# Sparse attention reordered: selection behind the index keys, a score bank per query tile, transposed weights, sums over 512 queries

## The reference

```
c_q, c_kv, k_idx, w_idx = split(h @ w_in)       # 256, 256, 64, 8 columns; c_q, c_kv, k_idx normed
q_abs, q_idx = split(c_q @ w_uq)                # 16 heads x 256 (normed), 8 index heads x 64
act   = relu(einsum("bqhd,bsd->bqhs", q_idx, k_idx) * 64 ** -0.5)
score = einsum("bqh,bqhs->bqs", w_idx, act)     # -1e30 where the key's chunk is ahead of the query's
sel   = top_k(score, 128)                       # one set of keys for all heads
logits = q_abs . c_kv[sel] * 256 ** -0.5 + bias[rel]
p      = softmax(logits)                        # masked as above
o      = (p @ c_kv[sel]) @ w_uv[head]           # 64 columns a head
h      = h + o @ w_out
```

## Time and profile before

| | us |
|---|---|
| median of three runs | 4014.04 (4010.49 to 4017.86) |
| the profiled execution | 4015.53 |
| its span on the core | 4013.8 |
| PE busy | 3690.2 (92%), 20688 records |
| PE weight loads busy | 2999.4 (75%) |
| DVE busy | 1743.2 (43%) |
| ACT busy | 1305.5 (33%) |
| POOL busy | 353.8 (9%) |
| PE's granted clock, mean of the core | 0.961 of full speed |

### The profile page before, as it was taken

The page is one execution under the profiler, slowest core; times in us unless marked ns, Lnnn a source line. Parts: engine busy times, 40 slices in busy tenths (PEclk is TensorE's granted clock), DMA queues, the critical chain, the costliest instruction groups (busy, mean ns, idle before and its releaser), DMA issues. The chain is left out here.

```text
span 4013.8 us, 51945 instructions
## 1 busy us (share of the span) xinstructions
PE 3690.2 (92%) x20688; PEld 2999.4 (75%) x20688; DVE 1743.2 (43%) x2625; ACT 1305.5 (33%) x1827; POOL 353.8 (9%) x263
## 2 busy tenths in 40 slices
PE   8999799699999998858888999999988989799997
PEld 7999677699999998425554888888833467677886
DVE  4442366354334432254332543444248843445432
ACT  4331366243324321123332442343110044324421
POOL 0000222000000000001000000000027332230000
PEclk9999899799999999969999999999989999899999
DMA  4322311022222223000002222322222242133221
GB/s 167 125 81 84 113 48 53 14 102 94 79 99 84 94 83 113 29 12 26 1 1 74 94 95 92 106 94 88 79 69 76 69 123 64 70 109 115 94 86 70
DMA packets 115310, 318.10 MB, mean 79 GB/s; under 512 B 13335, under 2 KB 56471, under 8 KB 99060
## 3 DMA queue, kind: packets, MB, share of 16 engines
q1 hardware_dynamic: 115188, 316.48, 23.2%
HBM read 307.95 MB, written 17.01 MB: 81 GB/s over the span
## 5 line engine op out<-in xcount | busy, mean ns | idle before, releaser
L326 PE MATMUL acc<-fb_xh,fb_wh 128*128 128x264 f32 x1408 | 287.9, 286 | 11.9 <-DVE fb_wl L476 11.9
L326 PE MATMUL acc<-fb_xl,fb_wh 128*128 128x264 f32 x1408 | 288.4, 286 | 0.0
L326 PE MATMUL acc<-fb_xh,fb_wl 128*128 128x264 f32 x1408 | 287.8, 286 | 0.0
L326 PE MATMUL acc<-fd_xh,fd_wh 128*128 128x512 f32 x704 | 275.8, 392 | 10.4 <-DVE fd_wl L476 10.4
L326 PE MATMUL acc<-fd_xh,fd_wl 128*128 128x512 f32 x704 | 274.8, 390 | 0.0
L326 PE MATMUL acc<-fd_xl,fd_wh 128*128 128x512 f32 x704 | 274.8, 390 | 0.0
L326 PEld LDWEIGHTS acc<-fb_xh,fb_wh 128*128 128x128 f32 x1408 | 220.1, 189 | 12.3 <-DVE fb_wl L476 12.1
L326 PEld LDWEIGHTS acc<-fb_xl,fb_wh 128*128 128x128 f32 x1408 | 219.4, 189 | 0.0
L326 PEld LDWEIGHTS acc<-fb_xh,fb_wl 128*128 128x128 f32 x1408 | 219.1, 189 | 0.0
L397 ACT ACTIVATE fb_wh<-fb_raw 128x2048 fp32r<-128x2048 f32 (+1 forms) x74 | 124.7, 1686 | 290.0 <-PE acc L385 176.9
L471 DVE TENSOR_TENSOR fb_wl<-fb_raw,fb_wh 128x2048 fp32r<-128x2048 f32 (+1 forms) x74 | 148.3, 2004 | 141.3 <-ACT fb_wh L397 140.5
(11 more groups left out here) (537 smaller groups left out, 8716.8 us busy)
## 6 DMA issues: line engine op xcount, KB each, us to landing
fb_raw<-wi_dram SPq DMA_DIRECT2D x42, 1024.0 KB, 4.8
fd_raw<-wi_dram SPq DMA_DIRECT2D x42, 1024.0 KB, 4.8
fb_raw<-wo_dram SPq DMA_DIRECT2D x32, 704.0 KB, 4.0
fd_raw<-wo_dram SPq DMA_DIRECT2D x32, 704.0 KB, 4.0
fa_raw<-wi_dram SPq DMA_DIRECT2D x20, 1024.0 KB, 4.8
ff_raw<-wi_dram SPq DMA_DIRECT2D x20, 1024.0 KB, 4.8
a_raw<-a_qkv_dram SPq DMA_DIRECT2D x24, 512.0 KB, 4.1
s_gw<-gate_w_dram SPq DMA_DIRECT2D x24, 512.0 KB, 4.0
```

The lines of the kernel that those rows point to most:

```text
L326: last = pe.matmul(acc[:, up_base(p, b) + 2 * a + q, 0:w], x[:, k, a, :], part[:, k, t0:t0 + w], start=k == 0 and part is xh and x is wv, ...
```

## The change

In `latents` the values are no longer computed; `uv` is loaded into the not yet used `mix` buffer in the same place of SP's queue. In `latent_heads`:
- The index jobs are placed by tile (`INDEX_AT`): tile 0 ahead of head 0; six jobs of tile 1 ahead of head 2 and two ahead of head 3; tile 2 at heads 5 and 7; tile 3 at heads 10, 11 and 12. There are four relu slots, not two. The 16 rounds of a selection are written out; there is no hardware loop.
- The scores of tile t stand in bank t. The first four are issued behind the last query, and then scores(g+4) behind turn(g). The ten value jobs stand between the last sums and the first turn, on ACT behind the root of the norms, all copied by ACT.
- The exponential is written over the logits, DVE scales them in place by the reciprocal (`weigh`, now behind logit(g+1)), and `turn` is a transpose of each key tile. Key tiles are now 16 meta keys and full tiles of 128. ACT's exps run three steps ahead, behind `spread`.
- `outputs` runs once a head, over 512 queries: the meta keys, then key tile j for the queries from 128 j on. ACT stores 64 x 512 at once.

```diff
-                    pe.wait_ge(there_uv, 17)
-                    pe.wait_ge(ckv_on, 2)
-                    for n, (j, rows, half) in enumerate(blocks):
...
+            AHEAD = 6
+            INDEX_AT = {0: (0, of_tile[1]), 2: (of_tile[1], of_tile[1] + AHEAD), 3: (of_tile[1] + AHEAD, of_tile[2]),
+                        5: (of_tile[2], of_tile[2] + AHEAD), 7: (of_tile[2] + AHEAD, of_tile[3]),
+                        10: (of_tile[3], of_tile[3] + AHEAD), 11: (of_tile[3] + AHEAD, of_tile[3] + 9),
+                        12: (of_tile[3] + 9, len(jobs))}
             I_BANK = (4, 5, 6)
-            OUT_BANK = (4, 5)
-            per_head = -(-len(jobs) // 8)
+            V_BANK = (5, 6)
+            T_BANK = (5, 7)
+            O_BANK = 6
+            OUT_BANK = (0, 1)
+            v_jobs = [(j, half) for j in range(-1, QT) for half in range(2)]
...
+                    def values(n):
+                        j, half = v_jobs[n]
+                        rows, at = (META, 0) if j < 0 else (P, META + j * P)
+                        if n >= 2:
+                            pe.wait_ge(v_ev, 1 + n - 1)
...
-                                last = pe.matmul(flat[:, 2 * BANK * (g % 2) + a:2 * BANK * (g % 2) + b],
+                                last = pe.matmul(flat[:, BANK * t + a:BANK * t + b],
...
                     def turn(g):
...
-                            last = pe.matmul(to, e[:, g % 2, j * P:j * P + n], diag[:, g % 2, :], start=True, stop=True)
+                        if t == NT - 1 and hd:
+                            pe.wait_ge(mixed, 1 + hd)
+                        pd, bank = lg_of(g), T_BANK[g % 2]
+                        to = acc[0:META, bank, (t + 1) * P:(t + 2) * P] if t < NT - 1 else acc[0:META, O_BANK, 0:P]
+                        pe.transpose(to, pd[:, 0:META], ident[:, :])
+                        for j in range(t + 1):
+                            last = pe.transpose(acc[:, bank, j * P:(j + 1) * P], pd[:, META + j * P:META + (j + 1) * P],
+                                                ident[:, :])
...
+                    def outputs(hd):
...
+                        pe.wait_ge(pt_ready, 1 + NT * (hd + 1))
+                        pe.matmul(acc[0:64, O_BANK, :], valm[:, hs], ptm[0:META, u, :], start=True, stop=False)
+                        for j in range(QT):
+                            last = pe.matmul(acc[0:64, O_BANK, j * P:], vals[:, j, hs], pt[:, u, j, j * P:],
+                                             start=False, stop=j == QT - 1)
...
+                    for hd in range(B_HEADS):
+                        for n in range(*INDEX_AT.get(hd, (0, 0))):
+                            index_scores(n)
+                        query(hd)
+                        if hd:
+                            sums(hd - 1)
+                    pe.wait_ge(q_ev, 1 + B_HEADS)
+                    pe.wait_ge(relued, 1 + len(jobs))
+                    for t in range(NT):
+                        scores(t)
+                    sums(B_HEADS - 1)
+                    pe.wait_ge(uv_there, 17)
+                    for n in range(len(v_jobs)):
+                        values(n)
+                    pe.wait_ge(v_ev, 1 + len(v_jobs))
+                    for g in range(LAST):
                         hd, t = STEPS_[g]
                         turn(g)
-                        if g + 2 < LAST:
-                            scores(g + 2)
-                        if g:
-                            outputs(g - 1)
+                        if g + NT < LAST:
+                            scores(g + NT)
+                        if t == 0 and hd:
+                            outputs(hd - 1)
...
-                        if n >= 2:
-                            act.wait_ge(i_added, 1 + n - 1)
+                        if n >= 4:
+                            act.wait_ge(i_added, 1 + n - 3)
...
                     act.wait_ge(u_mean, 2)
                     act.activation(rq[:, :, :], mean_u[:, :, :], ACT.Sqrt).then_inc(u_root, 1)
+                    for n in range(len(v_jobs)):
+                        take_values(n)
+                    for g in range(3):
+                        exps(g)
+                    for g in range(LAST):
                         hd, t = STEPS_[g]
                         spread(g)
+                        if t == 1 and hd:
+                            store(hd - 1)
+                        if g + 3 < LAST:
+                            exps(g + 3)
+                    store(B_HEADS - 1)
...
-                        with dve.Fori(0, TOPK // 8):
+                        for _round in range(TOPK // 8):
...
-                        dve.tensor_scalar(diag[:, s, :], ident[:, :], rden[:, s:s + 1], None,
-                                          ALU.mult).then_inc(weights, 1)
+                        dve.tensor_scalar(lg, lg, rden[:, s:s + 1], None, ALU.mult).then_inc(weights, 1)
...
                     logit(0)
-                    logit(1)
-                    for g in range(LAST):
-                        weigh(g)
-                        if g + 2 < LAST:
-                            logit(g + 2)
+                    for g in range(1, LAST):
+                        logit(g)
+                        weigh(g - 1)
+                    weigh(LAST - 1)
```

More of the change, by code:

```diff
@@ L1382, in _, with latent_heads @@
                     last.then_inc(ckv_on, 1)
[L1383 to L1389, removed]
+        def latent_heads(st, ckv, vals, valm, g_lat, widx, eps_q, mb, mix, uv, bw, c_bw, early, uq_there, uv_there):
             q_all = sb(st, "l_q_all", [P, 2 * B_HEADS, SEQ])
-            late = sb(st, "l_late", [P, 6 * SEQ])
             top8 = sb(st, "l_top8", [P, 8])
@@ L1404, in latent_heads @@
[L1404 to L1409, removed]
+            nmx = sb(st, "l_nmx", [P, 8])
@@ L1475, in index_scores @@
                                   kidx[hs, a:b], start=True, stop=True).then_inc(i_mm, 1)
[L1477 to L1480, removed]
-                        for n in range(per_head * hd + per_head // 2, min(len(jobs), per_head * (hd + 1))):
-                            index_scores(n)
-                        if hd:
-                            sums(hd - 1)
-                    sums(B_HEADS - 1)
+                    def values(n):
[3 more added lines that the diff above has]
+                            pe.wait_ge(v_ev, 1 + n - 1)
+                        for r in range(2):
+                            last = pe.matmul(acc[0:rows, V_BANK[n % 2], :], ckv[:, r, at:at + rows],
+                                             uv[:, 8 * half:8 * half + 8, r * 64:(r + 1) * 64],
+                                             start=r == 0, stop=r == 1)
+                        last.then_inc(v_mm, 1)
                     def scores(g):
@@ L1563, in _, with take_values @@
                         last.then_inc(q_ev, 1)
-                        for n in range(per_head * hd + per_head // 2, min(len(jobs), per_head * (hd + 1))):
+                    def take_values(n):
+                        j, half = v_jobs[n]
+                        cols = slice(512 * half, 512 * half + 512)
+                        act.wait_ge(v_mm, 1 + n + 1)
+                        if j < 0:
+                            act.activation(valm[:, cols], acc[0:META, V_BANK[n % 2], :], ACT.Copy).then_inc(v_ev, 1)
+                        else:
+                            act.activation(vals[:, j, cols], acc[:, V_BANK[n % 2], :], ACT.Copy).then_inc(v_ev, 1)
```

189 lines of the change are left out of this document (91 added, 98 removed).

## The result

The changed kernel takes 3842.41 us (median of 4 runs, 3838.15 to 3844.69) where the kernel before took 4014.51 (4 runs). The ratio is 0.957, 95% interval 0.9554 to 0.9587: faster by 172 us. The forecast was 3861, so the sign, the places and most sizes were right, and 19 us more came than were promised. The profiled execution is one of 3844.69 us, span 3843.0 (before 4015.53, span 4013.8), 170.8 less.

What follows compares the result with a forecast made beforehand. PE is busy nearly everywhere, so only the front (DVE its engine) and head loop (PE waiting for DVE) could pay: 4015.5 - 50.6 (front and values) - 102 (loop) = 3862.9, less 1.5 to the median, 3861; range 3842 to 3892.

Steps and rivals of the forecast that it cites:

- the loop's sum of PE a head: Head loop: PE alone sets the pace, scores 5.6, transposes 2.34, outputs 3.2, together 11.14 us a head; loop -102.
- rival B: Front: relus ahead block ACT, query takes wait, DVE keeps 29 us more of waits; near 3890, chance 0.11.
- The lower bound of 162: Head loop: its length in us with no handoff gaps at all, against 174.4 forecast.
- Values out of the latents: Before the front: without the value product, the query stage starts 21.4 us earlier, at about 1661.4.
- DVE's chain in the front: Front: rounds, additions, clearing, thresholds and 7.5 us of waits end selection 115.6 us after the stage's start.
- PE in the front: Front: queries, index jobs, half clock and stops about 104 us, 110 with first scores and last sums; done before DVE.
- The seam: Between selection and head loop: root, value jobs and first exp put the first turn at 134.3 us, 136.3 with half clock.
- A: DVE's selection rounds: the 0.34 gap is the replace draining, so unrolling gives nothing; 3877, chance 0.12.
- C: Head loop: stays bound by the chain, PE keeps its 46.5 us of waits for DVE; 3908, chance 0.11.
- D: Head loop: transposes let the clock fall to 1.2 GHz throughout, slower than before; 4034, chance 0.03.

Runs made afterwards that it cites:

- the run with wide weights: Changed kernel with the turn as matmuls with the identity, the first of each turn taking 128 weight columns instead of 16: 3866.24 us.
- the even placement: Changed kernel with index jobs and relus placed as in the kernel before, five a head over the first eight heads: 3870.67 us.
- the shallow lead: Changed kernel with scores issued two steps ahead instead of four, and exps two ahead instead of three: 3964.04 us.

## Why the prediction was right in kind and 19 us too slow

**The step that failed is the loop's sum of PE a head, 11.14 where 9.76 was measured.** Its transposes were sized right at 0.11, but 0.2 a group was added for a handoff that isn't there: turns 1.54, not 2.34. The scores were copied start to start from the earlier trace rows, 5.6, and take 4.92 without any change to them. Outputs were 0.1 too low, 3.2 for 3.30. The first two contain the same thing. In the kernel before nearly every neighbour has weights of another shape (128*128 in scores and turn, 128*16 at a turn's end, 128*64 and 16*64 in outputs), and each such seam costs 0.10 to 0.14 us in the runs above. Its trace had the row that shows it, beside the first scores of the earlier trace rows:

```profile
1969.09 0.76 PEld L1493 LDWEIGHTS acc<-b_ckv,l_q_all 128*128 128x128 f32 x4 [0.21 <-issue]
```

Load and matmul both start at 1969.09. I had read this "issue" as a price of each group. The 0.2 for a group of transposes came from the earlier trace rows in the same way. The 0.53 runs from the first load, 0.11 ahead of its matmul, to a load of another shape (64*128), which has this "issue" too:

```profile
494.75 0.27 PE L755 MATMUL acc<-ident,a_pd 128*16 128x128 f32 x1
```

Between transposes and scores the change made those seams free: the next load starts 0.11 or more ahead, also where 16 columns follow 128. Three seams a head remain around the outputs, the last one from 128*64 to a transpose, where load and matmul both start at 1836.64. The kernel before was not itself run with equal shapes, so that its 0.68 in the scores is seams rests on the row, the three times of the 272-key tile and the run with wide weights. The difference, 1.38 x 16 = 22, less a start and an end 4 us longer than summed, is the 18 missing in the loop. Two small sums in the forecast are off as well and decide nothing here: PE's terms in the front add up to 102, not 104, and rival B's extra waits to 32.5, not 29. The lower bound of 162 was set under the words "no handoff gaps at all" but kept 5.6 for the scores; the measured 156.3 lies below it, and with it the whole time is at the range's lower edge. The Trainium skill (Perfetto Trace Analysis, Tensor Engine Instruction) says that weights can be loaded to a background buffer and that this isn't investigated thoroughly; these runs show when the load is seen and when not.

**Values out of the latents:** right, 22.3 for 21.4.

**DVE's chain in the front:** right, 115 for 115.6 (the threshold at 1774.80 and 0.7 behind it, from 1660.5); its waits are 10.8 for the 7.5 followed, and the rounds a little shorter than summed.

**PE in the front:** 112 from the stage's start to the first value job (1772.57) for 110; stops of 5.9 in head 6 for 7, and 1.4 in all before queries 10 and 12 for 5, yet 2 us more in sum. I wrote that PE is done before DVE. It is, but by 3 us only, and with the even placement it is 14.6 behind.

**The seam:** 133.2 from the stage's start to the first turn for 134.3, without the 2 us of half clock that I added. These small terms make the front 4 us better than said.

**Depth instead of transposes:** the forecast gave PE the pace without asking what each part is worth. By the runs, two steps ahead cost 122, transposes save 40, outputs over 512 queries 16, the unrolled rounds 19, the placement 28. They don't add up, since each is measured beside all the others. Outputs over 512 queries were dismissed in the forecast as saving only handoffs, which is what they do; they are worth 16 all the same.

**Rivals.** A (unrolling gains nothing) is refuted: the gap is 0.08 in unrolled rounds and the run with the loop is 19.1 slower. By the Trainium skill's 0.11 us for a compare-and-branch (Advanced Engine Details and Errata, Control Flow Timing) the estimate was 7; the loop's end costs 0.26 here. B (the ring stays) and C (the loop waits for DVE) are what the even placement and the shallow lead show when one takes the cure away; the change doesn't have them. D (half clock from transposes) is refuted: 14 transposes a head among matmuls stand at a granted clock of 1.00 over 110 us. The Trainium skill (TensorE: Matmul & The Clock Gate, Part 4: PE-mode transpose) says that full clock doesn't engage for transposes; as a warning for this loop it did not hold, and no run here has a stage of transposes alone. Low clocks stood in loops with gaps: 0.85 with PE busy in 196 of 283 us, and 0.83 with matmuls in the transposes' place and PE busy in 242 of 328.

**Where 4 us stayed.** The two stages save 174.6, the span 170.8. The gate matmuls of the mixer's scan, in code that nothing here touches, last 252.6 us from first to last start (2788.0 to 3040.6) where they lasted 248.1, with records up to 1222 ns instead of 697. In three of the experiments they last 248.2 too, in the other profiled runs 252 to 253, whatever was edited there. The start of the stage, which no edit to the changed kernel touches either, lies between 1655.9 and 1661.0 in its traces. Together these are of the size of the 4 to 8 us between runs of one kernel; that they make them up is not shown, as only one run of each has a trace.

## What to carry to other kernels

When the same matmuls stand among new neighbours, don't copy their start-to-start times: take columns, and add a seam wherever the shape of the weights changes; the row of the weight load tells which seams are shown. Ask first how many steps of lead the longest chain needs: one step short cost 20 us here, all in waits, and two steps short 122, in waits and in clock. Where two engines end a stage within a few us of each other, count both, for each edit that helps one makes the other the bound.

## What the runs showed of the hardware beyond that

- fp32 matmuls of unlike weights shapes (128*16 to 128*128, 128*128 to 16*64, 16*64 to 128*64) start 0.10 to 0.14 us late, their load not hidden. Between equal shapes, and between 128*128 and a transpose of 16 columns, the load is hidden, 0.11 us ahead; a transpose behind 128*64 starts together with its load (1836.64). Turns of 128-wide weights cost 16.7 us less than with one 16-wide of each, though they load more.
- An fp32 transpose of 128 columns is one record of 0.11 us, a matmul with the identity two, 0.22 together.
- A 528-key round loses 0.26 us at the end of DVE's hardware loop (1.90 against 1.63).
- The clock went with gaps more than with kinds of work: 1.00 over 110 us without a gap, 0.85 and 0.88 over the loop with scores two ahead. Gaps alone don't set it: the kernel before had 1.00 from 1870 to 1960 with PE busy in 75.9 of 90 us, and one program had 0.52 and 0.83 over the same 20 us in two executions.
- A turn behind an idle wait of 1.61 us took 0.22 us, as without a wait; the one behind 1.54 took 1.03 instead of 0.55.
